# The norm between two projections on Trainium2: broadcast without a diagonal matrix, last squares in halves, and a new order on VectorE and ScalarE

## The chip, the cores and the metric

One core of one Trainium2 chip runs the whole program once. The metric is the device time of that execution in microseconds (us). Weights lie in HBM when it starts and are streamed in.

## What is computed

Two layers of a decoder trunk on 512 tokens of width 1024 in float32. Layer 0 mixes tokens with a Mamba-2 block, layer 1 with differential attention; each mixer is followed by a gated MLP with a short causal convolution. Every one of the four blocks is wrapped in two norms, and its output is added to the residual x:

```python
def rmsnorm(x, g):
    y = xf * lax.rsqrt(jnp.mean(xf * xf, axis=-1, keepdims=True) + RMS_EPS)
    return y * g

for i in range(2):
    hn = rmsnorm(x, norm_mix_pre[i])
    m = mamba2_mixer(hn, ...) if i % 2 == 0 else diff_attention(hn, ...)
    x = x + rmsnorm(m, norm_mix_post[i])
    hn = rmsnorm(x, norm_ffn_pre[i])
    f = conv_ffn(hn, ...)          # w_up: 1024 -> 5632, w_down: 2816 -> 1024
    x = x + rmsnorm(f, norm_ffn_post[i])
```

## The kernel before

Everything is kept transposed: a tensor of width 1024 is eight pieces of 128 features (partitions) by 512 tokens. Products are made in three parts, because float32 is split into a high and a low half (type float32r): hi x hi, hi x lo, lo x hi. `product` (L391) issues these three matmuls of 128x128 weights by 128x512 activations, at L395 to L397. Weights arrive in units of 512 or 704 KB in two slots of `raw`; for each unit ScalarE makes the high half (`split_hi`, L334, w_hi or fx_hi or ax_hi) and VectorE, in the attention and Mamba phases in part GpSimd, the low half (`split_lo_dve`, L353).

There are eight projections, and between an output projection (SOUT, DN0, AOUT, DN1) and the next input projection (UP0, QKV, UP1, the three in `WIDE`) lies a boundary, b = 1, 2, 3; b = 4 is the end of the program. b = 0 is its beginning. Each engine has its own instruction list, written out by hand, and semaphores hold them together. At a boundary this happens, in the order of the data:

- The output projection leaves its pieces 0 to 7 in banks of PSUM. ScalarE squares each (`out_chunk_act`, L721, by `square`, L471) and copies it to `mbuf` (L726); GpSimd adds the squares of pieces 0 to 6 into `ssq` (L485 for the first, L487). In `out_halves` (L728) and `out_wholes` (L745) ScalarE's list sets these pieces among the weight halves of units that come later (`ahead`); in the last round the halves of the next phase's units 0 to 2 stand ahead of piece 6.
- TensorE sums over the features: `sum_stat` (L489) multiplies four blocks of `ssq` (L495) and, after a wait, four blocks of the last square (L499) with a column of 1/1024. A float32 matmul shows as two records.
- ScalarE takes the root of the [128, 4] result (L422); VectorE takes the reciprocal (`norm_diag`, L434) and writes a [128, 4 x 128] tile `diag` with it on the diagonals (L427); TensorE multiplies all-ones by it (`norm_bcast`, L455), which puts the factor of each token on all 128 partitions of `b_norm`.
- VectorE (`boundary_dve`, L612) goes through the eight pieces: scale `mbuf` by gain and `b_norm` (L625), add it to x (L641), make hn_lo (L615). ScalarE (`boundary_act`, L575) makes hn_hi from the new x (L587) and its square for the pre-norm (L471); GpSimd adds these squares (L487). VectorE's order is: scale 0, add 0, scale 1, add 1, low 0, scale 2, then for m from 2: scale m+1, add m, low m-1. Ahead of it stands the low half of unit 3.
- TensorE (`wide_start`, L544) starts on units 0 to 3 at once, in four banks. Of chunk 0 it takes the two matmuls with hn_hi of all four units (L554, L555), then those with hn_lo (L558); chunks 1 to 5 follow for four units each, then chunks 6 and 7 unit by unit in the order 2, 3, 0, 1. Behind unit 2 it does the sums of the pre-norm and behind unit 0 the broadcast. The pre-norm is applied later, on the products (r_pre, L597).

Units from 4 on follow in the plain way (`in_unit`). SP's queue loads `raw` for a unit once the low half two units earlier is made. At b = 4 four of the eight adds are done by GpSimd (L602), and SP's queue sends x out.

Of the kernel before, what the change touches and what calls it, by code (L numbers as in the profile page):

```python
# [23 lines left out]
P = 128  # L24
S = 512
# [78 lines left out]
def trunk(nc, x_in, w_mix, w_sout, w_up0, w_dn0, w_qkv, w_aout, w_up1, w_dn1, params, lam_in, out):  # L104
    ctx = ExitStack()
    with ctx:
# [24 lines left out]
        root = sb("root", [P, NB])  # L131
        spare = sb("spare", [P, 1])
        rcol = sb("rcol", [P, NB])
        diag = sb("diag", [P, NB, P])
        rcol_hi, rcol_lo = sb("rcol_hi", [P, NB], F32R), sb("rcol_lo", [P, NB], F32R)
        diag_hi, diag_lo = sb("diag_hi", [P, NB, P], F32R), sb("diag_lo", [P, NB, P], F32R)
        ones_r = sb("ones_r", [P, P], F32R)
# [100 lines left out]
        dve_done = sem("dve_done")  # L238
        consts = sem("consts")

        sq_ready, sq_added = sem("sq_ready"), sem("sq_added")
        stat_ready, root_ready, diag_ready, bc_ready = (
            sem("stat_ready"), sem("root_ready"), sem("diag_ready"), sem("bc_ready"))
        rpre_copied = sem("rpre_copied")
# [42 lines left out]
            n += {"group": NG, "head": NH}.get(name, 1)  # L287

        sum_no = {name: n for n, name in enumerate(x for x in order if x not in ("group", "head"))}

        def gain(layer, kind, m):
            c = NORM0 + (layer * 4 + kind) * KC + m
# [131 lines left out]
        def norm_diag(dve, n, split=False):  # L424

            def on_diagonal(dst, r):
                return nc.vector.tensor_tensor(dst[:], ident[:].unsqueeze(1).to_broadcast([P, NB, P]),  # L427
                                               r.unsqueeze(2).to_broadcast([P, NB, P]), ALU.mult)

            dve.wait_ge(root_ready, n + 1)  # L430
            if not (isinstance(n, int) and n < 1):
                dve.wait_ge(diag_ready, n)
                dve.wait_ge(bc_ready, n)
            ch(nc.vector.reciprocal(rcol[:], root[:]))  # L434
            dve.wait_ge(dve_done, ch.value())
            if split:
                ch(nc.vector.tensor_copy(rcol_hi[:], rcol[:]))
                dve.wait_ge(dve_done, ch.value())
                ch(nc.vector.tensor_tensor(rcol_lo[:], rcol[:], rcol_hi[:].bitcast(F32), ALU.subtract))
                ch(on_diagonal(diag_hi, rcol_hi[:].bitcast(F32)))  # L440
                dve.wait_ge(dve_done, ch.value())
                on_diagonal(diag_lo, rcol_lo[:].bitcast(F32)).then_inc(diag_ready, 1)
            else:
                on_diagonal(diag, rcol[:]).then_inc(diag_ready, 1)

        def norm_bcast(pe, n, split=False):

            pe.wait_ge(diag_ready, n + 1)
            if split:
                nc.tensor.matmul(b_norm[:], ones_r[:], diag_hi[:].rearrange("p b t -> p (b t)"),  # L450
                                 start=True, stop=False)
                nc.tensor.matmul(b_norm[:], ones_r[:], diag_lo[:].rearrange("p b t -> p (b t)"),
                                 start=False, stop=True).then_inc(bc_ready, 1)
            else:
                nc.tensor.matmul(b_norm[:], ones[:], diag[:].rearrange("p b t -> p (b t)"),  # L455
                                 start=True, stop=True).then_inc(bc_ready, 1)

        def norm_before(n):

# [29 lines left out]
        def sum_stat(pe, name):  # L489

            n = sum_no[name]
            pe.wait_ge(sq_added, (KC - 1) * (n + 1))

            for b in range(NB):
                nc.tensor.matmul(b_norm[:, b:b + 1], ssq[:, b * P:(b + 1) * P], mean_col[:, 0:1],  # L495
                                 start=b == 0, stop=False)
            pe.wait_ge(sq_ready, KC * (n + 1))
            for b in range(NB):
                last = nc.tensor.matmul(b_norm[:, b:b + 1], sq[:, (KC - 1) % 2, b * P:(b + 1) * P],  # L499
                                        mean_col[:, 0:1], start=False, stop=b == NB - 1)  # L500
            last.then_inc(stat_ready, 1)
# [42 lines left out]
        def wide_start(pe, b, nxt):  # L544

            def chunk(j, c):
                return product(first_acc(nxt, j), 0, c, hn_hi[:, c, :], hn_lo[:, c, :], c == 0, c == KC - 1,
                               halves_of(nxt, j, True))

            pe.wait_ge(hnhi_ready, KC * b + 1)  # L550
            for j in range(4):
                pe.wait_ge(lo_made, nxt.U0 + j + 1)
                wh, wl = halves_of(nxt, j, True)
                nc.tensor.matmul(first_acc(nxt, j), wh[:, 0:P], hn_hi[:, 0, :], start=True, stop=False)  # L554
                nc.tensor.matmul(first_acc(nxt, j), wl[:, 0:P], hn_hi[:, 0, :], start=False, stop=False)  # L555
            pe.wait_ge(hnlo_ready, KC * b + 1)
            for j in range(4):
                nc.tensor.matmul(first_acc(nxt, j), halves_of(nxt, j, True)[0][:, 0:P], hn_lo[:, 0, :],  # L558
                                 start=False, stop=False)
            for c in range(1, KC - 2):  # L560
                pe.wait_ge(hnlo_ready, KC * b + c + 1)
                for j in range(4):
                    chunk(j, c)
            for n, j in enumerate((2, 3, 0, 1)):
                for c in (KC - 2, KC - 1):
                    pe.wait_ge(hnlo_ready, KC * b + c + 1)
                    last = chunk(j, c)
                last.then_inc(unit_done, 1)
                if n == 0:
                    wait_x_scaled(pe, b)  # L570
                    sum_stat(pe, f"pre{b}")
                elif n == 2:
                    norm_bcast(pe, norm_no[f"pre{b}"])
# [38 lines left out]
        def boundary_dve(dve, b, nxt=None):  # L612
            def lo(m):
                dve.wait_ge(hnhi_ready, KC * b + m + 1)
                nc.vector.scalar_tensor_tensor(hn_lo[:, m, :], x[:, m, :], gain(*GAINS[b][1], m),  # L615
                                               hn_hi[:, m, :].bitcast(F32), ALU.mult, ALU.subtract
                                               ).then_inc(hnlo_ready, 1)

            if b:
                norm_diag(dve, norm_no[f"post{b}"])  # L620
                if nxt is not None:
                    split_lo_dve(dve, nxt, 3)
                dve.wait_ge(bc_ready, norm_no[f"post{b}"] + 1)
            def scale(m):
                ins = nc.vector.scalar_tensor_tensor(mbuf[:, m, :], mbuf[:, m, :], gain(*GAINS[b][0], m),  # L625
                                                     b_norm[:], ALU.mult, ALU.mult)
                if m in POOL_ADDS[b]:
                    ins.then_inc(scaled, 1)
                else:
                    ch(ins)  # L630
                    made[m] = ch.value()

            made = {}
            if b:
                scale(0)
            for m in range(KC):
                if b and 1 < m and m + 1 < KC:
                    scale(m + 1)
                if b and m not in POOL_ADDS[b]:
                    dve.wait_ge(dve_done, made[m])  # L640
                    nc.vector.tensor_tensor(x[:, m, :], x[:, m, :], mbuf[:, m, :], ALU.add).then_inc(x_new, 1)  # L641
                if b and m == 0:
                    scale(1)
                if m and GAINS[b][1] is not None:
                    lo(m - 1)
                if b and m == 1:
                    scale(2)
            if GAINS[b][1] is not None:
                lo(KC - 1)
                if b:  # L650
                    split_lo_dve(dve, nxt, 4)
                norm_diag(dve, norm_no[f"pre{b}"])
                if not b:
                    split_lo_dve(dve, nxt, 2)
                dve.wait_ge(rpre_copied, b + 1)
# [65 lines left out]
        def out_chunk_act(act, ph, m, rep, b, units_before):  # L721

            act.wait_ge(unit_done, ph.U0 + units_before)
            acc = sout_acc(m) if ph is SOUT and isinstance(m, int) and m < 4 else acc_of(ph, rep)
            square(act, sum_no[f"post{b}"], m, rep, acc[:]).then_inc(sq_ready, 1)
            nc.scalar.activation(mbuf[:, m, :], acc[:], ACT.Copy).then_inc(evac["out"], 1)  # L726

        def out_halves(eng, ph, i, split, chunk, last=False):  # L728
# [5 lines left out]
            ahead(split, eng, ph, 4 * i + 4, 4)  # L734
            if last:
                ahead(split, eng, ph, 4 * i + 5, 5)
                ahead(split, eng, ph, 4 * i + 6, 6)
            chunk(2 * i, 0, 4 * i + 3)
            if last:
                chunk(2 * i + 1, 1, 4 * i + 4)  # L740
            else:
                ahead(split, eng, ph, 4 * i + 5, 5)
# [2 lines left out]
        def out_wholes(eng, ph, i, split, chunk, last=False):  # L745
            ahead(split, eng, ph, 2 * i + 2, 2)
            if last:
                ahead(split, eng, ph, 2 * i + 3, 3)
                ahead(split, eng, ph, 2 * i + 4, 4)
            chunk(2 * i, 0, 2 * i + 1)  # L750
            if last:
                chunk(2 * i + 1, 1, 2 * i + 2)
            else:
                ahead(split, eng, ph, 2 * i + 3, 3)
# [1099 lines left out]
```

## Time and profile before

| | |
|---|---|
| median of 3 runs | 1522.05 us (1521.98 to 1523.62) |
| profiled execution | 1520.41 us |
| its span, first to last instruction | 1518.4 us |
| TensorE matmul busy | 1460.5 us, 96% |
| VectorE busy | 1021.9 us, 67% |
| ScalarE busy | 613.2 us, 40% |
| GpSimd busy | 192.4 us, 13% |
| mean granted TensorE clock | 0.983 |

Times in the rows are microseconds from the start of the span. PE is TensorE's matmul row, DVE is VectorE, ACT ScalarE, POOL GpSimd. In brackets at the end of a row stands the idle time of that engine before the instruction and what ended it. Boundary 1 lies around 462 to 497, boundary 2 around 844 to 878, boundary 3 around 1120 to 1155, and the last one begins at 1502.

### The profile page before, as it was taken

Reading aid. Unit: us, or ns where it says so; the run is one execution under the profiler, and the core shown is the slowest. Engines: PE = TensorE matmul, PEld = TensorE weight load, DVE = VectorE, ACT = ScalarE, POOL = GpSimd, SP = SyncE. Lnnn points to the kernel's source line nnn. Section 1 sums busy time; section 2 is a strip of 40 time slices with the busy share of each in tenths; the row PEclk is TensorE's granted clock in tenths of the full one; section 3 lists DMA queues with packets and bytes.
Section 4 is the critical chain, followed back from the end, with each engine's and each line's share of the span. In section 5 each row is a group of like instructions: output and inputs, shape, how many; then the busy total and the mean of one; then the engine's idle time right before and its main releaser. Section 6 shows DMA issues by size and latency. Waiting matters only on the chain.

```text
span 1518.4 us, 20441 instructions
## 1 busy us (share of the span) xinstructions
PE 1460.5 (96%) x6774; PEld 1162.1 (77%) x6774; DVE 1021.9 (67%) x1428; ACT 613.2 (40%) x953; POOL 192.4 (13%) x123
## 2 busy tenths in 40 slices
PE   6999999999998999999999999999789999999996
PEld 5778888888786788888888767776568888888885
DVE  6888898889427787778422667778357877776223
ACT  5654555557324323322322436565443332233221
POOL 3011100111113000000011332222121000000111
PEclk9999999999999999999999999999889999999998
DMA  4433323332221222223322121111121322223221
GB/s 150 156 125 124 138 98 137 124 138 70 84 90 63 98 97 86 94 97 105 103 95 86 54 70 56 69 55 55 42 97 56 97 97 97 95 87 112 95 95 55
DMA packets 36277, 142.10 MB, mean 94 GB/s; under 512 B 4048, under 2 KB 4176, under 8 KB 34192
## 3 DMA queue, kind: packets, MB, share of 16 engines
q1 hardware_dynamic: 36240, 141.62, 27.1%
q8 instruction: 21, 0.34, 0.1%
q14 instruction: 16, 0.13, 0.0%
HBM read 139.38 MB, written 2.23 MB: 93 GB/s over the span
## 4 chain that ended last, share of the span: by engine, by line
PE 75%; issue 10%; DVE 7%; POOL 3%; ACT 3%; DMA 1%; DVEq 0%; SPq 0%; POOLq 0%; ACTq 0%
PE bank L395 17%; PE bank L396 16%; PE bank L397 16%; PE b_x L395 6%; PE b_x L397 6%; PE b_x L396 6%; POOL w_lo L350 3%; DVE w_lo L358 1%; DVE cv_s L812 1%; PE b_y L828 1%; ACT w_hi L344 1%; PE b_y L395 1%; PE b_y L396 1%; PE b_y L397 1%; PE b_x L840 1%
## 5 line engine op out<-in xcount | busy, mean ns | idle before, releaser
L358 DVE TENSOR_TENSOR w_lo<-raw,w_hi 128x1024 fp32r<-128x1024 f32 (+1 forms) x190 | 254.4, 1339 | 290.4 <-ACT w_hi L344 290.2
L344 ACT ACTIVATE w_hi<-raw 128x1024 fp32r<-128x1024 f32 (+1 forms) x211 | 233.5, 1107 | 467.1 <-PE bank L397 332.3
L395 PE MATMUL bank<-hn_hi,w_hi 128*128 128x512 f32 x872 | 352.8, 405 | 15.0 <-DVE hn_lo L615 10.8
L396 PE MATMUL bank<-hn_lo,w_hi 128*128 128x512 f32 x872 | 346.8, 398 | 0.0
L397 PE MATMUL bank<-hn_hi,w_lo 128*128 128x512 f32 x872 | 346.7, 398 | 0.0
L395 PEld LDWEIGHTS bank<-hn_hi,w_hi 128*128 128x128 f32 x872 | 165.2, 189 | 58.3 <-issue 12.7
L397 PEld LDWEIGHTS bank<-hn_hi,w_lo 128*128 128x128 f32 x872 | 165.2, 189 | 40.0
L396 PEld LDWEIGHTS bank<-hn_lo,w_hi 128*128 128x128 f32 x872 | 165.4, 190 | 37.8
L395 PE MATMUL b_x<-hn_hi,w_hi 128*128 128x512 f32 x362 | 143.4, 396 | 0.0
L397 PE MATMUL b_x<-hn_hi,w_lo 128*128 128x512 f32 x362 | 143.2, 395 | 0.0
L396 PE MATMUL b_x<-hn_lo,w_hi 128*128 128x512 f32 x362 | 143.1, 395 | 0.0
L397 PE MATMUL bank<-h_hi,w_lo 128*128 128x512 f32 x352 | 139.2, 396 | 0.0
L395 PE MATMUL bank<-h_hi,w_hi 128*128 128x512 f32 x352 | 139.2, 396 | 0.0
L396 PE MATMUL bank<-h_lo,w_hi 128*128 128x512 f32 x352 | 139.2, 396 | 0.0
L487 POOL TENSOR_TENSOR ssq<-ssq,sq 128x512 f32<-128x512 f32 x48 | 83.4, 1738 | 250.4 <-ACT sq L471 250.0
L485 POOL COPY ssq<-sq 128x512 f32<-128x512 f32 x8 | 9.2, 1149 | 599.8 <-ACT sq L471 599.8
L395 PEld LDWEIGHTS b_x<-hn_hi,w_hi 128*128 128x128 f32 x362 | 68.0, 188 | 16.6
L397 PEld LDWEIGHTS b_x<-hn_hi,w_lo 128*128 128x128 f32 x362 | 68.0, 188 | 16.5
L396 PEld LDWEIGHTS b_x<-hn_lo,w_hi 128*128 128x128 f32 x362 | 68.0, 188 | 16.1
L396 PEld LDWEIGHTS bank<-h_lo,w_hi 128*128 128x128 f32 x352 | 66.1, 188 | 16.1
L395 PEld LDWEIGHTS bank<-h_hi,w_hi 128*128 128x128 f32 x352 | 66.1, 188 | 16.1
L397 PEld LDWEIGHTS bank<-h_hi,w_lo 128*128 128x128 f32 x352 | 66.1, 188 | 15.9
(248 smaller groups left out, 2120.1 us busy)
## 6 DMA issues: line engine op xcount, KB each, us to landing
raw<-w_up SPq DMA_DIRECT2D x88, 512.0 KB, 3.2
raw<-w_mix SPq DMA_DIRECT2D x49, 512.0 KB, 3.3
raw<-w_dn SPq DMA_DIRECT2D x32, 704.0 KB, 4.0
raw<-w_qkv SPq DMA_DIRECT2D x24, 512.0 KB, 3.3
acs_bc<-scratch SPq DMA_DIRECT2D x8, 1024.0 KB, 5.3
ecs_bc<-scratch SPq DMA_DIRECT2D x8, 1024.0 KB, 4.7
raw<-w_sout SPq DMA_DIRECT2D x16, 512.0 KB, 3.3
raw<-w_aout SPq DMA_DIRECT2D x8, 512.0 KB, 3.4
```

The source lines that it names most:

```text
L344: nc.scalar.activation(halves_of(ph, rep, first and j < 2)[0], raw[:, slot, 0:ph.width], ACT.Copy).then_inc(hi_made, 1)
L350: nc.gpsimd.tensor_tensor(w_lo[:, slot, 0:ph.width], raw[:, slot, 0:ph.width], w_hi[:, slot, 0:ph.width].bitcast(F32), ALU.subtract).then_ ...
L358: nc.vector.tensor_tensor(lo, raw[:, slot_of(ph, rep), 0:ph.width], hi.bitcast(F32), ALU.subtract).then_inc(lo_made, 1)
L395: nc.tensor.matmul(acc[:], wh, hi, start=first, stop=False)
L396: nc.tensor.matmul(acc[:], wh, lo, start=False, stop=False)
L397: return nc.tensor.matmul(acc[:], wl, hi, start=False, stop=last)
L485: nc.gpsimd.tensor_copy(ssq[:], sq[:, 0, :]).then_inc(sq_added, 1)
L487: nc.gpsimd.tensor_tensor(ssq[:], ssq[:], sq[:, rep % 2, :], ALU.add).then_inc(sq_added, 1)
L812: ins = nc.vector.scalar_tensor_tensor(dst, ug[:, t:t + S], col(wcol + t), dst, ALU.mult, ALU.add)
L828: last = nc.tensor.matmul(dst, xdt[:, c, hh, :], m_t[:, hh, c * P:(c + 1) * P], start=True, stop=c == 0)
L840: last = nc.tensor.matmul(b_x[:, c // 2, (c % 2) * 2 * P:(c % 2) * 2 * P + 2 * P], btok[:, c, :], xdd[:, c, :, :].rearrange("p h d -> p (h ...
```

## The change

- `norm_diag`: where the factor isn't split (all norms but those of the groups and heads), VectorE makes the reciprocal only; `diag` is gone. `norm_bcast` issues four matmuls whose stationary operand is one column of `rcol` repeated 128 times and whose moving operand is the identity, 128 columns each.
- `out_chunk_act`: the square of piece 7 is made in two halves of 256 tokens, each with a semaphore; `sum_stat` of a post-norm takes the first two blocks after the first half, the last two after the second.
- `out_halves`, `out_wholes`: in the last round ScalarE takes piece 6 ahead of the high half of the next phase's unit 2.
- `boundary_dve` for b = 1 to 3: scale 0, add 0, scale 1, add 1, low 0, low 1, low half of weight unit 3, scale 2; then for m from 2: add m, scale m+1, low m. The low half of weight unit 3 no longer stands ahead of scale 0.
- `wide_start`: chunks 0 and 1 are done for units 0 to 2 first, then for unit 3; from chunk 2 on all four units go together.

```diff
@@ norm_diag
+            if not split:
+                nc.vector.reciprocal(rcol[:], root[:]).then_inc(diag_ready, 1)
+                return
             ch(nc.vector.reciprocal(rcol[:], root[:]))
...
-            else:
-                on_diagonal(diag, rcol[:]).then_inc(diag_ready, 1)
@@ norm_bcast
-                nc.tensor.matmul(b_norm[:], ones[:], diag[:].rearrange("p b t -> p (b t)"),
-                                 start=True, stop=True).then_inc(bc_ready, 1)
+                for b in range(NB):
+                    last = nc.tensor.matmul(b_norm[:, b * P:(b + 1) * P], rcol[:, b:b + 1].to_broadcast([P, P]),
+                                            ident[:], start=True, stop=True)
+                last.then_inc(bc_ready, 1)
@@ sum_stat
+            post = name in norms_post
...
-            pe.wait_ge(sq_ready, KC * (n + 1))
             for b in range(NB):
+                if post and b == 0:
+                    pe.wait_ge(sq_half, norms_post.index(name) + 1)
+                if b == (NB // 2 if post else 0):
+                    pe.wait_ge(sq_ready, KC * (n + 1))
@@ wide_start
-            for j in range(4):
+            for j in range(3):
                 pe.wait_ge(lo_made, nxt.U0 + j + 1)
...
             pe.wait_ge(hnlo_ready, KC * b + 1)
-            for j in range(4):
+            for j in range(3):
...
-            for c in range(1, KC - 2):
+            pe.wait_ge(hnlo_ready, KC * b + 2)
+            for j in range(3):
+                chunk(j, 1)
+            pe.wait_ge(lo_made, nxt.U0 + 4)
+            for c in range(2):
+                chunk(3, c)
+            for c in range(2, KC - 2):
@@ boundary_dve
                 norm_diag(dve, norm_no[f"post{b}"])
-                if nxt is not None:
-                    split_lo_dve(dve, nxt, 3)
                 dve.wait_ge(bc_ready, norm_no[f"post{b}"] + 1)
...
+            def add(m):
+                dve.wait_ge(dve_done, made[m])
+                nc.vector.tensor_tensor(x[:, m, :], x[:, m, :], mbuf[:, m, :], ALU.add).then_inc(x_new, 1)
...
+            if nxt in WIDE:
+                for m in range(2):
+                    scale(m)
+                    add(m)
+                for m in range(2):
+                    lo(m)
+                split_lo_dve(dve, nxt, 3)
+                scale(2)
+                for m in range(2, KC):
+                    add(m)
+                    if m + 1 < KC:
+                        scale(m + 1)
+                    lo(m)
+                split_lo_dve(dve, nxt, 4)
+                norm_diag(dve, norm_no[f"pre{b}"])
+                dve.wait_ge(rpre_copied, b + 1)
+                return
@@ out_chunk_act
-            square(act, sum_no[f"post{b}"], m, rep, acc[:]).then_inc(sq_ready, 1)
+            if isinstance(m, int) and m == KC - 1:
+                act.wait_ge(sq_added, (KC - 1) * sum_no[f"post{b}"] + m - 1)
+                for half, done in ((0, sq_half), (1, sq_ready)):
+                    cols = slice(half * S // 2, (half + 1) * S // 2)
+                    nc.scalar.activation(sq[:, rep % 2, cols], acc[:, cols], ACT.Square).then_inc(done, 1)
+            else:
+                square(act, sum_no[f"post{b}"], m, rep, acc[:]).then_inc(sq_ready, 1)
@@ out_halves, and out_wholes in the same way
                 ahead(split, eng, ph, 4 * i + 5, 5)
-                ahead(split, eng, ph, 4 * i + 6, 6)
             chunk(2 * i, 0, 4 * i + 3)
             if last:
+                ahead(split, eng, ph, 4 * i + 6, 6)
                 chunk(2 * i + 1, 1, 4 * i + 4)
```

## Rows read from the trace of the kernel before

**Rows 1.** The page, busy time of TensorE: us, share of the span, instructions.

```profile
PE 1460.5 (96%) x6774; PEld 1162.1 (77%) x6774; DVE 1021.9 (67%) x1428; ACT 613.2 (40%) x953; POOL 192.4 (13%) x123
```

**Rows 2.** Timeline around boundary 2: start, duration, engine, line, op, out<-in, count.

```profile
829.24 0.40 PE L395 MATMUL bank<-h_hi,w_hi 128*128 128x512 f32 x1
...
843.71 0.40 PE L397 MATMUL bank<-h_hi,w_lo 128*128 128x512 f32 x1
843.94 0.95 PE L495 MATMUL b_norm<-mean_col,ssq 128*128 128x1 f32 x8
...
846.39 0.69 DVE L427 TENSOR_TENSOR diag<-ident,rcol 128x512 f32<-128x512 f32 x1
...
847.14 1.12 PE L455 MATMUL b_norm<-diag,ones 128*128 128x512 f32 x2 [1.29 <-DVE diag L427]
...
848.30 0.75 DVE L625 SCALAR_TENSOR_TENSOR mbuf<-mbuf,par,b_norm 128x512 f32<-128x512 f32 x1
```

**Rows 3.** Timeline of boundary 2, the stretch behind the first scale.

```profile
850.58 0.80 PE L554 MATMUL b_y<-hn_hi,ax_hi 128*128 128x512 f32 x1 [2.32 <-ACT hn_hi L587]
...
851.08 0.74 DVE L615 SCALAR_TENSOR_TENSOR hn_lo<-x,par,hn_hi 128x512 fp32r<-128x512 f32 x1
...
851.19 1.10 POOL L485 COPY ssq<-sq 128x512 f32<-128x512 f32 x1 [10.25 <-ACT sq L471]
...
866.25 2.45 DVE L615 SCALAR_TENSOR_TENSOR hn_lo<-x,par,hn_hi 128x512 fp32r<-128x512 f32 x2
...
878.04 0.39 PE L395 MATMUL bank<-hn_hi,w_hi 128*128 128x512 f32 x1
```

**Rows 4.** Timeline of boundary 1, TensorE.

```profile
461.78 0.40 PE L397 MATMUL bank<-y_hi,w_lo 128*128 128x512 f32 x1
462.72 1.02 PE L495 MATMUL b_norm<-mean_col,ssq 128*128 128x1 f32 x8 [0.55 <-POOL ssq L487]
...
465.93 1.46 PE L455 MATMUL b_norm<-diag,ones 128*128 128x512 f32 x2 [1.29 <-DVE diag L427]
```

**Rows 5.** Timeline of boundary 3, TensorE.

```profile
1119.49 0.40 PE L397 MATMUL bank<-o_hi,w_lo 128*128 128x512 f32 x1
...
1120.47 1.02 PE L495 MATMUL b_norm<-mean_col,ssq 128*128 128x1 f32 x8 [0.59 <-POOL ssq L487]
```

**Rows 6.** Timeline of boundary 2, VectorE, ScalarE and GpSimd at pieces 2 to 4.

```profile
855.64 0.68 DVE L641 TENSOR_TENSOR x<-x,mbuf 128x512 f32<-128x512 f32 x1
...
855.82 1.66 POOL L487 TENSOR_TENSOR ssq<-ssq,sq 128x512 f32<-128x512 f32 x1 [1.97 <-ACT sq L471]
856.24 1.78 DVE L615 SCALAR_TENSOR_TENSOR hn_lo<-x,par,hn_hi 128x512 fp32r<-128x512 f32 x1
856.36 0.73 ACT L587 ACTIVATE hn_hi<-x,par 128x512 fp32r<-128x512 f32 x1 [0.68 <-DVE x L641]
...
856.99 0.62 ACT L471 ACTIVATE sq<-x 128x512 f32<-128x512 f32 x1
...
857.75 1.43 POOL L487 TENSOR_TENSOR ssq<-ssq,sq 128x512 f32<-128x512 f32 x1 [0.27 <-ACT sq L471]
...
857.95 0.73 DVE L625 SCALAR_TENSOR_TENSOR mbuf<-mbuf,par,b_norm 128x512 f32<-128x512 f32 x1
...
858.61 1.12 DVE L641 TENSOR_TENSOR x<-x,mbuf 128x512 f32<-128x512 f32 x1
```

**Rows 7.** Timeline of TensorE, four float32 matmuls of 128 columns in the Mamba phase.

```profile
361.61 1.06 PE L859 MATMUL b_cb<-cT,bT 128*128 128x128 f32 x8
```

**Rows 8.** Windows: stretch, its length, each engine's busy time, granted clock, DMA share, GB/s.

```profile
469.80:473.40 3.60, 3.60 (x9) 2.82 (x10) 3.60 (x5) 1.63 (x3) 2.39 (x2) 0.50 0.03 13
...
1122.00:1128.30 6.30, 2.74 (x6) 1.08 (x5) 4.25 (x7) 1.92 (x4) 0.00 (x0) 0.50 0.25 84
```

**Rows 9.** Timeline of GpSimd and of VectorE in the Mamba phase.

```profile
139.15 1.39 POOL L1001 TENSOR_TENSOR yt<-yt 128x512 f32<-128x512 f32 x1 [33.02 <-ACT yt L927]
...
139.31 2.31 DVE L358 TENSOR_TENSOR w_lo<-raw,w_hi 128x1024 fp32r<-128x1024 f32 x1
```

More of the change, by code:

```diff
@@ L133, in trunk @@
         rcol = sb("rcol", [P, NB])
-        diag = sb("diag", [P, NB, P])
         rcol_hi, rcol_lo = sb("rcol_hi", [P, NB], F32R), sb("rcol_lo", [P, NB], F32R)
@@ L239, in trunk @@
         consts = sem("consts")
-        sq_ready, sq_added = sem("sq_ready"), sem("sq_added")
+        sq_ready, sq_added, sq_half = sem("sq_ready"), sem("sq_added"), sem("sq_half")
         stat_ready, root_ready, diag_ready, bc_ready = (
@@ L289, in trunk @@
         sum_no = {name: n for n, name in enumerate(x for x in order if x not in ("group", "head"))}
+        norms_post = [f"post{b}" for b in range(1, 5)]
         def gain(layer, kind, m):
@@ L433, in norm_diag @@
                 dve.wait_ge(bc_ready, n)
+            if not split:
+                nc.vector.reciprocal(rcol[:], root[:]).then_inc(diag_ready, 1)
+                return
             ch(nc.vector.reciprocal(rcol[:], root[:]))
             dve.wait_ge(dve_done, ch.value())
[L436 to L442, printed above, removed]
-            else:
-                on_diagonal(diag, rcol[:]).then_inc(diag_ready, 1)
+            ch(nc.vector.tensor_copy(rcol_hi[:], rcol[:]))
+            dve.wait_ge(dve_done, ch.value())
+            ch(nc.vector.tensor_tensor(rcol_lo[:], rcol[:], rcol_hi[:].bitcast(F32), ALU.subtract))
+            ch(on_diagonal(diag_hi, rcol_hi[:].bitcast(F32)))
+            dve.wait_ge(dve_done, ch.value())
+            on_diagonal(diag_lo, rcol_lo[:].bitcast(F32)).then_inc(diag_ready, 1)
         def norm_bcast(pe, n, split=False):
@@ L748, in out_wholes @@
                 ahead(split, eng, ph, 2 * i + 3, 3)
-                ahead(split, eng, ph, 2 * i + 4, 4)
             chunk(2 * i, 0, 2 * i + 1)
             if last:
+                ahead(split, eng, ph, 2 * i + 4, 4)
                 chunk(2 * i + 1, 1, 2 * i + 2)
```

## The prediction

> **What bounds the kernel now.** I read the page first: TensorE is busy for 96% of the span [rows 1]. So only its gaps count, and those that this change touches are four: one after each output projection (b = 1, 2, 3 and the last, 4), where a norm must be finished before the next products can start. The timeline of b = 2 shows such a gap in full [rows 2]: the last product starts at 843.71, the sums of squares follow on TensorE (L495, L499), then the root on ScalarE, the reciprocal and the diagonal on VectorE, the broadcast on TensorE (L455), and VectorE begins to scale at 848.30. I call that start S0. The first product of the new phase starts 2.28 later, at 850.58, and the first product of weight unit 4 at 878.04 [rows 3], which is 29.74 after S0. In those 29.74 lie 96 products for units 0 to 3, at 0.2334 each (829.24 to 843.71 are 62 of them [rows 2]): 22.4 if nothing holds them.
>
> The view to look at longest is VectorE beside GpSimd inside that stretch [rows 6]. For each of the eight pieces of x VectorE scales (S, L625, reads PSUM), adds (A, L641) and makes the low half (L, L615), and GpSimd adds one square (L487). An L or an A beside a GpSimd add grows: L takes 1.78 where it took 0.74 [rows 3], A 1.12 instead of 0.68, and each ends about 0.54 after GpSimd (857.48 and 858.02, 859.18 and 859.73). GpSimd in its turn ends 1.16 after the A or L that it found running (856.32 and 857.48, 858.02 and 859.18). S beside it stays at 0.73. So A, L and the GpSimd add exclude each other, and S fits beside them. With these constants the whole stretch can be worked out: from 848.30 I get the end of the last L at 868.6, and the trace has 868.70 [rows 3].
>
> **The front of the gap: what is gained.**
> *Output six first.* At b = 1 L495 starts at 462.72, held by GpSimd's add, although the last product started at 461.78 [rows 4]; at b = 2 it starts 0.23 behind the last product. The add is late because ScalarE squares output six only behind the weight halves of the next phase. With the order changed the square and the add are over before the last product, so L495 starts at 462.01: 0.71 gained. At b = 3, 1120.47 against 1119.49 + 0.23: 0.75 [rows 5]. At b = 2 L495 waits for nothing [rows 2], and b = 4 has no weights ahead: 0.
> *Squares in halves.* The eight records of L495 last 0.95 [rows 2], 0.11 from one to the next, and the whole square is ready about when they are through: I count 0.04 at b = 2 and 4. No row has a 256-wide square: two of them take between 0.6 (the whole one, split) and 1.2 (twice the whole), and the second is wanted 0.44 after the first (four records), so 0 to 0.1 could be lost. The copy of that bank comes later by as much, hidden: the root stands a microsecond off.
> *No diagonal.* L427 takes 0.69 and its wait 0.04: 0.73 between the reciprocal and L455 at all four posts. In its place TensorE issues four 128-wide products for one of 512. The nearest row is four such fp32 products, eight records, in 1.06 [rows 7]; L455 takes 1.12 at b = 2 [rows 2], 1.46 at b = 1, where the clock fell inside it [rows 4], and at b = 3 the clock was down before it began [rows 8]. No row has a stationary operand repeated from one column. Bounds: 0.06 less to 0.9 more for each broadcast, if such a load took twice as long; I take 1.06. In the four pre-norms the broadcast stands in TensorE's queue behind products, and the diagonal was hidden under those: 0 to 0.1 each.
> S0 comes earlier by 0.71 + 0.73 + 0.40 = 1.84 at b = 1; by 0.73 + 0.06 + 0.04 = 0.8 at b = 2 and at 4; at b = 3 by 0.75 + 0.73 = 1.5, and up to 1.0 more if the broadcast now meets the full clock, I take 2.2. Sum: 5.7.
> The low half of unit 3 (w_lo, L358) leaves the front too. It lay beside the broadcast and ended with it: S0 follows the end of L455 (848.26) by 0.04 [rows 2], so this brings no more.
>
> **The stretch behind S0: what is lost.** For b = 1 to 3 the new order is S0 A0 S1 A1 L0 L1, w_lo of unit 3, S2, and then A(m) S(m+1) L(m). Before, an L belonged to the piece before, so it never waited for ScalarE. Now L(m) waits for hn_hi(m). Counted from the end of A(m): hn_hi starts at 0.04 and takes 0.73, L starts at 0.80 and ends at 1.55. The square starts 0.63 behind hn_hi and takes 0.62, and GpSimd starts 0.14 later [rows 6], at 1.43: inside L(m), which A(m+1) follows directly, with its start at 1.47. If GpSimd is served first, it runs for 1.16, and A(m+1) ends 0.54 later: 1.55 + 1.16 + 0.54 = 3.25 a piece. The 12 products of a piece need 12 x 0.2334 = 2.80. VectorE becomes the bound.
> By the same constants, from S0: A1 ends at 2.84, L0 3.50, L1 4.53 (behind the GpSimd copy), w_lo of unit 3 6.76 (behind the first GpSimd add, which ends at 5.69), S2 7.42, A2 8.14, A7 8.14 + 5 x 3.24 = 24.3, L7 25.9 (it was 20.4). TensorE has 21 products left behind L7 (4.9), and the sums and the broadcast, 16 x 0.11 + 0.9 = 2.7: 33.5, against 29.74. Three times 3.8: 11.3 lost. (At b = 1 and 3 the old stretch may be somewhat shorter, since part of the 29.74 is products at half rate; I leave that in the range.)
> Unit 3 is now wanted by TensorE 18 products after its start at 2.27. At half rate for the 3.6 us of [rows 8] at b = 1 that is 8.1, later than 6.76: hidden, with 1.3 to spare. The load of unit 5 on SP's queue waits for that half and moves with it by some 5 us; TensorE wants unit 5 24 products after 878.04, some 20 us later: hidden. The new waits queue little: behind TensorE's wait for a half square stand only L499 and the broadcast, behind ScalarE's wait only the copy of the same bank; GpSimd splits no weights there.
>
> **The clock.** TensorE's products ran at 1.2 GHz (0.50) after the gaps [rows 8], 3.6 us of them at b = 1. That price is inside 29.74, and in the new stretch it is hidden, since VectorE sets the end. But the new stretch has a hole of its own: before L7 TensorE waits 2.5 us, and right before that stand only three products (0.7) and another wait of 0.4. At b = 3 the clock was down from 1122.0 on, 2.5 us behind the start of the last product, although small matmuls went on [rows 5, 8]. I estimate that half of the three holes bring it down, each for the 3.6 us seen, which costs 1.8: 2.6 added. All of them for twice as long would be 11.
>
> **Sum.** 11.3 - 5.7 + 2.6 = 8.2. The profiled execution took 1520.41 around a span of 1518.4; the median of the runs shown is 1522.05, 1.6 above it, and I add the sum to the median: 1530.3 us.
>
> **Rivals.**
> *GpSimd and VectorE take turns.* 1.43 and 1.47 are closer than any pair of rows: VectorE ahead by 0.11 goes first (851.08 and 851.19, its 0.74 unstretched [rows 3]), GpSimd ahead by 0.16 goes first too (139.15 and 139.31: w_lo then lasts 2.31, until 1.08 behind GpSimd [rows 9]). If A(m+1) wins at 0.04, GpSimd runs behind it and L(m+1) ends at 1.70; GpSimd's next start, 1.43, is then clearly ahead. A pair of pieces costs 2.3 + 3.2 = 5.5, or 2.77 each, just under 2.80. L7 ends at 23.0, the stretch is 30.6, 2.6 are lost in three against 5.7 gained: 1519.0, just inside what can't be told from none.
> *VectorE keeps ahead.* If the adds never fall onto A, a piece costs 1.55 + 0.60 = 2.15, TensorE waits for nothing, and the front's gain stays whole: 1522.05 - 5.7 = 1516.3. The point from which it decides is 2.80 a piece. Against it: in [rows 6] the old order, with more slack, has an A and an L stretched already.
> *The broadcast is dear.* At twice the load time the four posts lose 3.6, the four pre-norms as much: 1537.5 with the first case.
> The Trainium skill ("SBUF — State Buffer", section "Who interferes with whom") says that issue order decides, and that whoever issues first holds the shared pair for the whole instruction. The trace agrees at 0.11 and 0.16 and can't say at 0.04. By that rule GpSimd wins here too, which speaks for 1530 and not for 1519.
>
> **Chances.** GpSimd first 0.60, turns 0.17, VectorE ahead 0.18, dear broadcast 0.05. Faster by over 0.2% (3 us, about what a measurement of this kernel can tell from no change) is the third, 0.20 with a little of the second's lower edge; within it 0.18; slower 0.62. The range goes from 1516.5, nearly the whole front gain, to 1537.0, the first case with most of the clock's losses.
>
> **What would show it.** Right: L495 at b = 1 and 3 0.23 behind the last product; the broadcast 0.05 behind the reciprocal and 1.06 long; from m = 3 on A(m) about 1.8 long, a GpSimd add in front of each, and 3.2 from A to A; the last hn_lo ending near 26 after S0; TensorE waiting 2.5 us for it. Wrong: A of 0.68 and stretches of 29 to 30 us (then 1516 to 1519), or a broadcast near 2 us at full clock.

## The result and the profile after

The changed kernel takes 1541.64 us (median of 4 runs, 1539.69 to 1543.42) against 1522.01 for the kernel before: 1.0125 times, with a 95% interval of 1.0109 to 1.0141. By the medians it is slower by 19.6 us; 8.2 had been forecast, and the top of the range was 1537. The profiled execution took 1541.56 around a span of 1539.5.

The page of the changed kernel first (busy time, then the chain that ended last). TensorE's share is what it was in [rows 1]; in the chain VectorE now has 10%, where it had 7%.

```profile
PE 1474.7 (96%) x6822; PEld 1175.9 (76%) x6822; DVE 1024.3 (67%) x1420; ACT 613.1 (40%) x957; POOL 188.3 (12%) x123
...
PE 73%; issue 10%; DVE 10%; ACT 3%; POOL 3%; DMA 1%; DVEq 0%; SPq 0%; POOLq 0%; ACTq 0%
```

The front of boundary 2, timeline of the changed kernel; it answers to [rows 2] (L499 is the sum over `ssq`, L457 the new broadcast, L636 the first scale, S0).

```profile
849.21 0.40 PE L398 MATMUL bank<-h_hi,w_lo 128*128 128x512 f32 x1
...
849.44 0.95 PE L499 MATMUL b_norm<-mean_col,ssq 128*128 128x1 f32 x8
...
851.62 0.18 DVE L436 RECIPROCAL rcol<-root 128x4 f32<-128x4 f32 x1 [6.21 <-ACT root L423]
...
851.85 1.16 PE L457 MATMUL b_norm<-ident,rcol 128*128 128x128 f32 x8 [0.57 <-DVE rcol L436]
...
853.04 0.75 DVE L636 SCALAR_TENSOR_TENSOR mbuf<-mbuf,par,b_norm 128x512 f32<-128x512 f32 x1 [1.25 <-PE b_norm L457]
```

S0 stands 3.83 behind the start of the last product, where it was 4.59. The stretch behind it, which answers to [rows 6] (L628 the low half, L490 the GpSimd add, L646 the add to x, L636 the scale):

```profile
861.97 0.75 DVE L628 SCALAR_TENSOR_TENSOR hn_lo<-x,par,hn_hi 128x512 fp32r<-128x512 f32 x1
...
862.60 1.29 POOL L490 TENSOR_TENSOR ssq<-ssq,sq 128x512 f32<-128x512 f32 x1 [3.89 <-ACT sq L474]
862.64 1.79 DVE L646 TENSOR_TENSOR x<-x,mbuf 128x512 f32<-128x512 f32 x1
...
864.35 0.74 DVE L636 SCALAR_TENSOR_TENSOR mbuf<-mbuf,par,b_norm 128x512 f32<-128x512 f32 x1
864.47 0.72 ACT L600 ACTIVATE hn_hi<-x,par 128x512 fp32r<-128x512 f32 x1 [2.01 <-DVE x L646]
...
865.10 0.62 ACT L474 ACTIVATE sq<-x 128x512 f32<-128x512 f32 x1
865.22 0.75 DVE L628 SCALAR_TENSOR_TENSOR hn_lo<-x,par,hn_hi 128x512 fp32r<-128x512 f32 x1
...
865.86 1.29 POOL L490 TENSOR_TENSOR ssq<-ssq,sq 128x512 f32<-128x512 f32 x1 [1.97 <-ACT sq L474]
865.89 1.80 DVE L646 TENSOR_TENSOR x<-x,mbuf 128x512 f32<-128x512 f32 x1
```

From piece 3 on every GpSimd add starts 0.04 ahead of VectorE's add to x and goes first; the add to x takes 1.8 instead of 0.68, and one piece after the other costs 3.25 (862.64 to 865.89). The low half of weight unit 3 falls behind a GpSimd add in the same way, as in [rows 9]:

```profile
857.32 1.39 POOL L490 TENSOR_TENSOR ssq<-ssq,sq 128x512 f32<-128x512 f32 x1 [0.29 <-ACT sq L474]
...
857.50 2.29 DVE L359 TENSOR_TENSOR w_lo<-raw,w_hi 128x1024 fp32r<-128x1024 f32 x1
```

The last of the eight low halves ends 25.96 behind S0. Then the hole, TensorE alone, and the windows around it (stretch, length, busy times of TensorE's matmuls, its loads, VectorE, ScalarE and GpSimd, granted clock, DMA share, GB/s), which answer to [rows 8]:

```profile
876.38 0.40 PE L398 MATMUL b_x<-hn_hi,w_lo 128*128 128x512 f32 x1
879.06 0.50 PE L396 MATMUL b_x<-hn_hi,w_hi 128*128 128x512 f32 x1 [2.28 <-DVE hn_lo L628]
```

```profile
878.00:879.00 1.00, 0.00 (x0) 0.00 (x0) 0.74 (x1) 0.74 (x2) 0.00 (x0) 1.00 0.00 0
879.20:882.50 3.30, 3.30 (x20) 3.10 (x21) 1.28 (x2) 1.32 (x2) 0.00 (x0) 0.80 0.00 0
882.60:888.00 5.40, 5.40 (x16) 4.34 (x15) 0.01 (x1) 0.00 (x0) 1.70 (x3) 0.50 0.28 97
889.00:891.00 2.00, 2.00 (x10) 1.63 (x9) 1.61 (x3) 1.97 (x4) 0.00 (x0) 1.00 0.04 8
```

Three products of chunk 6, then 2.3 us of nothing, three products and the sums. Inside the sums, at 881.2, the clock falls to 0.50, and it stays there to 888.0, through most of the products of units 3, 0 and 1. At boundary 3 it falls sooner, at 1164.5, behind the same hole but before the sums (L499) begin; timeline and windows:

```profile
1164.09 0.50 PE L396 MATMUL b_x<-hn_hi,w_hi 128*128 128x512 f32 x1 [2.27 <-DVE hn_lo L628]
...
1165.23 1.70 PE L499 MATMUL b_norm<-mean_col,ssq 128*128 128x1 f32 x8
```

```profile
1161.90:1164.00 2.10, 0.00 (x0) 0.00 (x0) 1.31 (x2) 1.24 (x2) 0.04 (x1) 1.00 0.00 0
1164.50:1165.20 0.70, 0.70 (x3) 0.55 (x2) 0.00 (x0) 0.00 (x0) 0.00 (x0) 0.50 0.00 0
```

From these readings the 21.1 us between the two spans can be laid out. (It is more than the 19.6 of the medians, because the profiled execution of the kernel before was its fastest, 1.6 under its median.) A stretch is counted from S0 to the first product of unit 4.

| part | before | after | difference |
|---|---|---|---|
| stretches behind S0, b = 1, 2, 3 | 29.31, 29.73, 29.31 | 35.26, 36.83, 38.42 | +22.2 |
| last product to S0, b = 1 to 4 | 5.65, 4.59, 6.59, 4.58 | 4.76, 3.83, 4.20, 4.63 | -4.0 |
| attention phase, unit 4 of b = 2 to last product of b = 3 | 241.45 | 244.00 | +2.5 |
| start to last product of b = 1 | 461.78 | 462.22 | +0.4 |

The two feed-forward phases between them are equal to 0.01 us. The attention phase is no part of the change: it took between 241.5 and 244.7 in the profiles of the kernels below, with one or another stretch of low clock in it.

### The profile page after: what moved, and what is told of

Same layout as the page of the kernel before. It is cut to its first block, busy times and chain, and to the rows that moved or that the text cites. A ratio compares the mean times of both kernels' runs of the same rounds, so it can differ in the third digit from the quotient of the medians.

```text
span 1539.5 us, 20533 instructions
## 1 busy us (share of the span) xinstructions
PE 1474.7 (96%) x6822; PEld 1175.9 (76%) x6822; DVE 1024.3 (67%) x1420; ACT 613.1 (40%) x957; POOL 188.3 (12%) x123
## 4 chain that ended last, share of the span: by engine, by line
PE 73%; issue 10%; DVE 10%; ACT 3%; POOL 3%; DMA 1%; DVEq 0%; SPq 0%; POOLq 0%; ACTq 0%
PE bank L396 17%; PE bank L398 17%; PE bank L397 17%; PE b_x L396 5%; PE b_x L397 5%; PE b_x L398 5%; POOL w_lo L351 3%; DVE x L646 2%; DVE w_lo L359 2%; DVE cv_s L850 1%; DVE hn_lo L628 1%; ACT hn_hi L600 1%; DMA raw<-w_mix 1%; PE b_y L866 1%; DVE mbuf L636 1%
## 5 line engine op out<-in xcount | busy, mean ns | idle before, releaser
L359 DVE TENSOR_TENSOR w_lo<-raw,w_hi 128x1024 fp32r<-128x1024 f32 (+1 forms) x190 | 256.8, 1351 | 292.1 <-ACT w_hi L345 292.1
L396 PE MATMUL b_x<-hn_hi,w_hi 128*128 128x512 f32 x365 | 146.8, 402 | 7.4 <-DVE hn_lo L628 7.4
L490 POOL TENSOR_TENSOR ssq<-ssq,sq 128x512 f32<-128x512 f32 x48 | 79.4, 1655 | 260.4 <-ACT sq L474 260.0
```

What stands on the lines that cost most here:

```text
L359: nc.vector.tensor_tensor(lo, raw[:, slot_of(ph, rep), 0:ph.width], hi.bitcast(F32), ALU.subtract).then_inc(lo_made, 1)
L396: nc.tensor.matmul(acc[:], wh, hi, start=first, stop=False)
L490: nc.gpsimd.tensor_tensor(ssq[:], ssq[:], sq[:, rep % 2, :], ALU.add).then_inc(sq_added, 1)
```

## The experiments

Ratios are against the kernel before, run beside them, with 95% intervals; its medians there were 1523.34 (first four), 1523.33 (the filled hole) and 1523.50 (the last three).

### The front alone

```diff
 all of the change, but boundary_dve and wide_start as in the kernel before
```

> All of the change but the new order on VectorE and TensorE behind the first scale (boundary_dve and wide_start as before). Theory (order makes VectorE the bound): the front's gain stays, A(m) alternate 0.68 and 1.12 as before, last hn_lo 20.4 behind the first scale, stretch to unit 4 29.3 to 29.7; 1517 us, 5 under before. Rival (the front itself is dear: the halves, the piece-six order, the broadcast at half clock): over 1522, up to 1530.

1519.71 us, ratio 0.9975 (0.9963 to 0.9986): 3.8 us faster. The stretches were 29.74, 30.12 and 29.35, the last low half ended 20.4 behind S0, and the adds to x alternated between 0.68 and 1.12 as before. So nothing of the front is dear, but it gave less than the 5.7 of the sum. In the profile S0 came earlier by 1.15, -0.12, 2.09 and 0.75, where the sum had 1.84, 0.83, 2.2 and 0.83. At b = 2 the new broadcast met the low clock and took 2.03. The timeline at boundary 1 shows what is missing there (L457 the broadcast, L359 the low half of weight unit 3, L632 the first scale):

```profile
464.75 1.16 PE L457 MATMUL b_norm<-ident,rcol 128*128 128x128 f32 x8 [0.57 <-DVE rcol L436]
465.46 1.23 DVE L359 TENSOR_TENSOR w_lo<-raw,w_hi 128x1024 fp32r<-128x1024 f32 x1 [0.77 <-ACT w_hi L345]
466.61 0.74 DVE L632 SCALAR_TENSOR_TENSOR mbuf<-mbuf,par,b_norm 128x512 f32<-128x512 f32 x1
```

The broadcast is over at 465.91, but VectorE stands at the weight half until 466.69, since the high half of it comes from ScalarE only at 465.43. In the kernel before, the diagonal filled the time in which VectorE waited for that half. Without the diagonal, the weight half becomes what S0 waits for, 0.66 at b = 1; at b = 2 and 3, where the broadcast ran longer (2.03 and 1.70), it cost nothing and 0.12.

### The order alone

```diff
 the kernel before, with boundary_dve and wide_start of the change
```

> The kernel before with the new order alone (boundary_dve and wide_start of after). Theory: a piece costs 3.25 on VectorE, last hn_lo 26.0 behind the first scale, stretches 35 to 38 us: 1522 + 12 + 10 of clock = 1544, 1541 to 1548. Rival (front and order only hurt together): 1525 to 1535.

1544.03 us, ratio 1.0133 (1.0116 to 1.0150). The three stretches were 36.81, 36.79 and 36.81, and the last low half ended at 25.97, 25.96 and 25.98. The order alone makes all of the loss.

### GpSimd's adds cut short

```diff
 def add_square(pool, name, m, rep):
+    w = 32 if name in ("pre1", "pre2", "pre3") else S
...
-    nc.gpsimd.tensor_tensor(ssq[:], ssq[:], sq[:, rep % 2, :], ALU.add)
+    nc.gpsimd.tensor_tensor(ssq[:, 0:w], ssq[:, 0:w], sq[:, rep % 2, 0:w], ALU.add)
```

> The changed kernel, but GpSimd adds only 32 of 512 columns of the squares of the three pre-norms (their means are wrong for the other tokens). Order and waits are as in the change. Theory (A waits for the GpSimd add): A 0.68, a piece costs 2.15 to 2.3, last hn_lo at 18 to 20 behind the first scale, no hole on TensorE, stretches 29 to 30 us, 1516 to 1518. Rival (L waiting for hn_hi of its own piece makes the time): pieces stay over 2.8, over 1530.

1517.37 us, ratio 0.9958 (0.9944 to 0.9972); this kernel leaves out 480 of the 512 columns of those sums. The timeline at boundary 2 shows the same order and the same starts, with the GpSimd add (L491) 0.04 ahead, now 0.25 long:

```profile
857.67 0.25 POOL L491 TENSOR_TENSOR ssq<-ssq,sq 128x32 f32<-128x32 f32 x1 [1.97 <-ACT sq L474]
857.71 0.76 DVE L647 TENSOR_TENSOR x<-x,mbuf 128x512 f32<-128x512 f32 x1
...
859.89 0.25 POOL L491 TENSOR_TENSOR ssq<-ssq,sq 128x32 f32<-128x32 f32 x1 [1.97 <-ACT sq L474]
859.93 0.76 DVE L647 TENSOR_TENSOR x<-x,mbuf 128x512 f32<-128x512 f32 x1
```

A piece costs 2.22, the last low half ends at 19.65, and the stretches are 29.62, 30.01 and 30.16. The weight half takes 1.30 instead of 2.29, and the clock doesn't fall behind the last low half. So the change's order is slow because of the time that GpSimd holds in front of the weight half and of each add to x from piece 3 on (1.16 us each), and because of the hole that this makes. That L waits for the hn_hi of its own piece costs little or nothing on TensorE's path: these stretches lie within 0.1 of the range of those with the old order in the run above (29.35 to 30.12).

### Chunk 6 for all four units before chunk 7

```diff
-            for c in range(2, KC - 2):
+            for c in range(2, KC - 1):
...
             for n, j in enumerate((2, 3, 0, 1)):
-                for c in (KC - 2, KC - 1):
-                    pe.wait_ge(hnlo_ready, KC * b + c + 1)
-                    last = chunk(j, c)
+                pe.wait_ge(hnlo_ready, KC * (b + 1))
+                last = chunk(j, KC - 1)
```

> The changed kernel, but TensorE does chunk 6 for all four units before chunk 7, so only 12 products instead of 21 stand behind the last hn_lo, and its hole shrinks from 2.5 to 0.4 us. VectorE as in the change, last hn_lo at 26.0. If the holes bring the clock down and that is the 10 us that the sum missed: no clock loss behind the last hn_lo, stretches 31.4 to 31.6, 1522 to 1525. If something else takes them: 1534 to 1537, only the 2.1 per stretch of products moved ahead is gained.

1523.80 us, ratio 1.0001 (0.9991 to 1.0010). VectorE is as slow as in the change (25.96), but the stretches are 31.59, 31.59 and 31.58, and the clock holds behind the last low half at all three boundaries (windows, with the columns of the table above; the third number from the end is the clock):

```profile
490.00:498.00 8.00, 7.81 (x46) 6.53 (x46) 2.98 (x4) 2.98 (x5) 0.37 (x1) 1.00 0.11 33
872.00:881.00 9.00, 8.80 (x51) 7.35 (x50) 3.76 (x5) 3.58 (x6) 2.52 (x4) 1.00 0.16 52
1149.00:1159.00 10.00, 9.64 (x53) 7.89 (x53) 4.65 (x7) 3.93 (x7) 1.28 (x1) 1.00 0.16 51
```

This one edit in TensorE's order brings the time back to that of the kernel before. It doesn't undo the new order: the stretches are still 6.4 us longer together than those of the kernel before, and the front's gain makes up for most of that. In the profiles the three stretches are 15.7 shorter than in the change. Nine products of each were moved ahead of the wait, 2.1 each and 6.3 together; the other 9.4 are the clock's, unless moving the products did more than that, which the next run tests. The sums of the pre-norm stand behind the last low half here too, and the clock holds.

### The hole filled with idle work

To part the clock from the moved products, nine matmuls that nobody needs were put into the hole.

```diff
                 for c in (KC - 2, KC - 1):
+                    if n == 0 and c == KC - 1:
+                        for f in range(9):
+                            nc.tensor.matmul(b_norm[:], halves_of(nxt, 0, True)[0][:, 0:P], hn_hi[:, f % 6, :],
+                                             start=True, stop=True)
                     pe.wait_ge(hnlo_ready, KC * b + c + 1)
```

> The changed kernel with nine more matmuls at each of b = 1 to 3, of old data into a bank that nobody reads, issued by TensorE after chunk 6 of unit 2, in the 2.5 us in which it waits for the last hn_lo (9 x 0.234 = 2.1 us). Nothing else moves: 21 products still stand behind the last hn_lo, which comes at 26.0. If the hole costs by bringing the clock down: it stays at full rate, the stretches are 33.5 as the sum had them, instead of 35.3 to 38.4, and the kernel is 8 to 10 us faster with more work: 1530 to 1533. If the clock falls for another reason or the products themselves make the time: 1540 to 1544.

1531.71 us, ratio 1.0051 (1.0035 to 1.0068): 27 matmuls more, and some 10 us less than the change (by the medians 9.9, by the ratios 11). Timeline at boundary 2 (L581 is the idle work) and windows:

```profile
875.94 2.27 PE L581 MATMUL b_norm<-hn_hi,ax_hi 128*128 128x512 f32 x9
878.40 0.50 PE L396 MATMUL b_x<-hn_hi,w_hi 128*128 128x512 f32 x1 [0.19 <-DVE hn_lo L632]
```

```profile
490.00:500.50 10.50, 10.31 (x57) 8.54 (x57) 3.80 (x6) 3.58 (x6) 0.87 (x1) 1.00 0.15 51
877.00:887.50 10.50, 10.31 (x51) 8.41 (x50) 2.51 (x4) 3.46 (x6) 1.78 (x3) 0.84 0.14 51
1158.00:1168.00 10.00, 9.81 (x55) 8.10 (x55) 3.47 (x4) 3.07 (x6) 0.86 (x1) 1.00 0.17 54
```

The stretches are 33.68, 35.28 and 33.73, where the sum on record had 33.5. At b = 1 and 3 the clock held; at b = 2 it fell at 881.1, behind the sums, for 3.4 us. So filling the hole keeps the clock in two cases of three. Why it fell at b = 2 is open: behind the last low half the three boundaries show the same work, and what differs is the low clock at the front of the boundary, 10.2 us long there and 6.8 at the other two.

### The low half one piece behind

```diff
                 for m in range(2, KC):
-                    add(m)
                     if m + 1 < KC:
                         scale(m + 1)
-                    lo(m)
+                    add(m)
+                    if m > 2:
+                        lo(m - 1)
+                lo(KC - 1)
```

> The changed kernel, but from piece 2 on the low half is made one piece behind again: scale m+1, add m, low m-1; the low half of weight unit 3 stays after low 1. Theory (it is low m directly ahead of add m+1 that lets the GpSimd add fall onto every add): adds are no longer all 1.8; the constants give the last hn_lo at 22.5 behind the first scale (26.0 in the change, 20.4 before), stretches of 30.8 without the hole at the end, 1521 to 1523. Rival (the weight half in the middle of VectorE's order is what costs): the last hn_lo stays at 25 or more, over 1535.

1520.33 us, ratio 0.9977 (0.9966 to 0.9987). The adds to x at boundary 2 took 0.68, 0.68, 1.12, 1.11, 0.68 and 1.78; the last low half ended at 22.56 and the stretches were 30.82, 30.80 and 30.80. That is 0.7 under the range that I expected. So the order of adds and low halves is the cause. The weight half was not moved here, and what its place costs is in the next run.

### The weight half right behind the first add

```diff
+                scale(0)
+                add(0)
+                split_lo_dve(dve, nxt, 3)
+                scale(1)
+                add(1)
+                lo(0)
+                lo(1)
+                scale(2)
 ... then as in the one before
```

> As the one with the low half one piece behind, but the low half of weight unit 3 comes right after add 0. Nothing stands ahead of the first scale, so it should follow the broadcast by 0.04 (3.6 to 4.5 us behind the start of the sums, against 4.26 to 4.5 in the run with the old order, where VectorE was still at that weight half when the broadcast had ended). Constants: last hn_lo at 21.3, stretches 29.5 to 30.0. Theory: 1516 to 1518, some 1 to 2 under the run with the old order. Rival (the first scale isn't held by that weight half): the same as that run, 1519 to 1520.

1518.24 us, ratio 0.9968 (0.9956 to 0.9980), the best of the kernels that compute everything: by the ratio 4.9 us under the kernel before, and 0.2 over the range that I expected. Timeline at boundary 2:

```profile
845.02 1.16 PE L457 MATMUL b_norm<-ident,rcol 128*128 128x128 f32 x8 [0.57 <-DVE rcol L436]
846.22 0.75 DVE L636 SCALAR_TENSOR_TENSOR mbuf<-mbuf,par,b_norm 128x512 f32<-128x512 f32 x1 [1.25 <-PE b_norm L457]
...
847.61 1.22 DVE L359 TENSOR_TENSOR w_lo<-raw,w_hi 128x1024 fp32r<-128x1024 f32 x1
```

S0 follows the broadcast (846.18) by 0.04, as expected; the last low half ends at 21.4 and the stretches are 29.66, 29.63 and 29.67, 1.15 less than with the weight half behind low 1. That it beats the front alone isn't shown: the two intervals overlap.

### The new broadcast alone

```diff
 the kernel before, with norm_diag and norm_bcast of the change
```

> The kernel before with the new broadcast alone (no diagonal; low half of weight unit 3 still ahead of the first scale). By the sum on record each of the four posts gains 0.73 and more: 1522 - 3 = 1519. By the reading of the run with all of the front: at b = 1 to 3 VectorE must first make the low half of weight unit 3, whose high half is ready 1.2 behind the start of the root, so the first scale comes 2.5 behind the root with or without the diagonal, and only b = 4 gains 0.7: 1521 to 1522, no difference.

1520.16 us, ratio 0.9981 (0.9972 to 0.9990): by the ratio 2.9 us faster, 1.5 to 4.3, so the sum on record had the size and my later reading was too low. The place is partly the later reading's (L455 the broadcast, L357 the weight half, L626 the first scale, boundary 2):

```profile
846.41 1.16 PE L455 MATMUL b_norm<-ident,rcol 128*128 128x128 f32 x8 [0.57 <-DVE rcol L434]
847.12 1.23 DVE L357 TENSOR_TENSOR w_lo<-raw,w_hi 128x1024 fp32r<-128x1024 f32 x1 [0.77 <-ACT w_hi L343]
848.27 0.74 DVE L626 SCALAR_TENSOR_TENSOR mbuf<-mbuf,par,b_norm 128x512 f32<-128x512 f32 x1
```

The broadcast ends at 847.57, and S0 comes at 848.27, where it was 848.30 with the diagonal. From the start of the root to S0 it is 2.38, 2.38, 2.64 and 2.59 us; before, 2.75, 2.42, 3.37 and 2.42. Gained are 0.4 at b = 1 and 0.7 at b = 3, where the clock was down at the old broadcast. Over all four that is 1.0 of the 2.9. The rest can't be placed from this pair of profiles: their spans differ by only 0.3 us (1518.4 and 1518.1), since the profiled execution of the kernel before, at 1520.41, was the fastest of all of its runs.

## Why the prediction was wrong

The direction, the mechanism and its place were right. What failed is the size, and above all one term of the sum, the clock: 2.6 on record, 10.0 measured.

- *VectorE against GpSimd.* On record: A of 1.8, 3.25 a piece, the last low half 25.9 behind S0, w_lo of unit 3 behind the first GpSimd add. Measured: 1.78 to 1.80, 3.25 to 3.26, 25.95 to 25.97. That weight half took 2.29 where it had taken 1.23. The open question, who goes first at 0.04, was decided for GpSimd at all three boundaries in every piece from 3 on, 15 cases, so the two rivals in which VectorE wins are out. The rule of the Trainium skill ("SBUF — State Buffer", section "Who interferes with whom"), that issue order decides, agrees with the trace at 0.04 too. Cutting the adds short shows it from the other side. The loss, 33.5 a stretch, is 12.1 against the three measured stretches of before (I had 11.3, with 29.74 for all).
- *The clock: the step that failed.* On record: half of the three holes bring it down for 3.6 us, 2.6 together, all of them for twice as long 11. Measured: the stretches exceed 33.5 by 1.8, 3.3 and 4.9, 10.0 together; the clock fell at all three, for 3.4, 6.8 and 10.2 us. With the order alone it was 3.3 each time, 9.9. I had the upper bound written down and took a quarter of it, on one row (half of three times 1.8 is 2.7, not 2.6). The step that failed is the estimate that half of the holes bring the clock down, each for 3.6 us: all of them did, for 6.8 on average. With the hole (the change, the order alone) the clock fell at 6 of 6 boundaries. In the seven profiles that have no such hole it fell behind the last low half at none of 21, although the same sums, 1.8 us of small matmuls, stand there in every one. At b = 3 of the change it fell before the sums began. So the sums alone don't bring it down, and whether they add to what a hole does isn't shown. The filled hole and chunk 6 moved ahead both show that this term, and not a slower VectorE, is what was missing: 7.8 of the 10.0 come back in the profile of the one, and 9.4 beside the moved products in that of the other.
- *The range.* Its upper end took "most of the clock's losses"; with all of them it would have been 1530.3 - 2.6 + 11 = 1538.7, and the attention phase added 2.5 in the profiled run.
- *Output six first.* On record 0.71 and 0.75; L499 of the changed kernel starts 0.23 to 0.24 behind the last product at all four. Right.

The changed kernel at boundary 1, TensorE:

```profile
462.22 0.40 PE L398 MATMUL bank<-y_hi,w_lo 128*128 128x512 f32 x1
462.46 0.95 PE L499 MATMUL b_norm<-mean_col,ssq 128*128 128x1 f32 x8
...
464.87 2.08 PE L457 MATMUL b_norm<-ident,rcol 128*128 128x128 f32 x8 [0.56 <-DVE rcol L436]
```

- *The broadcast.* 1.16 at full clock at b = 2 against 1.12 for the old one (I had 1.06): a column repeated as stationary operand makes the load hardly dearer (0.1 for the four), and that rival is out. But at b = 1 and 4 the clock was down at the broadcast, and it took 2.08 and 1.95; S0 came earlier by 0.9 at b = 1, where 1.84 stood on record, and no earlier at all at b = 4. At b = 3 the clock fell inside it: 1.52 instead of 2.08, and S0 came 2.4 earlier (2.2 on record). The front gained 4.0 in this profile, 3.8 in the runs of the front alone, for 5.7 on record.
- *Halves.* The root follows the start of the sums by 1.88 instead of 1.94 to 1.95: 0.06, where 0.04 stood on record.
- *The weight half of unit 3.* I said that its leaving brings no more, since it ended with S0. That held only while the diagonal was there. With the diagonal gone it holds S0 up by 0.66 where the broadcast runs at full clock (b = 1 of the front alone, b = 1 and 2 of the new broadcast alone), and by 0 to 0.12 where the clock is down.

## What to carry to other kernels

When VectorE and GpSimd share a stretch, write down for each of VectorE's two-input instructions what GpSimd instruction becomes ready while the one before it runs: here a GpSimd start inside the low half took the place of the add behind it (1.80 for that add), and with a scale, which reads PSUM, between the two the add took 1.12 [rows 6]. An idle time of TensorE must be priced with the clock that it brings down: three holes of 2.3 us cost 10.0 more here. Work that is ready should be kept for such a hole (chunk 6 here), which brought the time back to that of the kernel before. And before an instruction is removed, see what else was waiting behind the same engine: the next one may take all of its time (848.27 against 848.30 for S0 at b = 2 of the new broadcast alone).

## What the hardware showed that I had not expected

A lead of 0.04 us (862.60 against 862.64) is enough for GpSimd, even while VectorE's instruction before is still running (861.97 + 0.75 = 862.72) and the next has already started. GpSimd then ends at 863.89, 1.17 behind that instruction, and the add to x at 864.43, 0.54 behind GpSimd: by these times GpSimd got in between two of VectorE's instructions that follow each other directly. And 27 needless matmuls made the program about 10 us faster.
